# The first two modulation groups in quarters of their outputs, columns picked by four identity columns, first k-slice modulated on VectorE

## The reference, cut to what matters

```
mod = silu(c) @ w_mod + b_mod                # c for latent tokens, c_ctx for context tokens
shift1, scale1, gate1, shift2, scale2, gate2 = split(mod, 6)     # 1024 values each
h = layer_norm_plain(x) * (1 + scale1) + shift1
z = h @ w_in                                 # first 768 columns are q, k, v
```

## Time and profile before

| | |
|---|---|
| median of 3 runs | 936.22 us (934.71 to 936.78) |
| the profiled execution | 939.29 us, its span 937.5 us |
| TensorE busy | 869.9 us, 93% of the span |
| VectorE, ScalarE, GpSimd busy | 773.4, 581.3 and 158.5 us |
| mean granted TensorE clock | 0.967 |
| DMA | 272.78 MB, mean 291 GB/s |

### The profile page before, as it was taken

How to read it: one execution, slowest core, us unless ns; L and a number is a source line. 1 busy time by engine, 2 the same in 40 slices (tenths; PEclk the granted TensorE clock), 3 DMA queues, 4 the chain that set the end, 5 groups by cost and what they waited for, 6 DMA issues and landing times.

```text
span 937.5 us, 12308 instructions
## 1 busy us (share of the span) xinstructions
PE 869.9 (93%) x4962; PEld 613.7 (65%) x4962; DVE 773.4 (82%) x808; ACT 581.3 (62%) x596; POOL 158.5 (17%) x107
## 2 busy tenths in 40 slices
PE   3899999688899947999999999999999999999995
PEld 3789977456678834666666666666666666666663
DVE  5388545877879876898989989998998998998877
ACT  1455266746732344777777777777777777677753
POOL 1000300010011033003303303303302311320220
PEclk9899999799999966999999999999999999999998
DMA  9920540452059296999999999999999999999716
GB/s 338 361 110 8 201 181 1 180 105 78 2 204 357 93 400 247 373 419 392 418 392 393 410 392 390 402 398 388 390 402 385 378 415 381 374 414 386 268 15 201
DMA packets 59348, 272.78 MB, mean 291 GB/s; under 512 B 6728, under 2 KB 7036, under 8 KB 42908
## 3 DMA queue, kind: packets, MB, share of 16 engines
q1 hardware_dynamic: 50848, 245.33, 67.1%
q0 software_dynamic: 7536, 24.00, 9.0%
q10 hardware_dynamic: 908, 2.68, 0.8%
HBM read 257.99 MB, written 14.00 MB: 290 GB/s over the span
## 4 chain that ended last, share of the span: by engine, by line
PE 85%; DVE 6%; ACT 3%; DMA 3%; issue 1%; SPq 0%; another core or an unknown queue 0%; ACTq 0%; DVEq 0%
PE PS L935 24%; PE PS L937 24%; PE PS L936 24%; PE PS L1122 1%; PE PS L1076 1%; DMA ring<-in_w_mod 1%; PE PS L1106 1%; PE PS L1145 1%; PE PS L1262 1%; PE PS L1275 1%; DMA acc_scratch<-ysc,idx_u 1%; PE PS L1198 1%; DVE smin L1609 1%; PE PS L951 1%; PE PS L961 1%
## 5 line engine op out<-in xcount | busy, mean ns | idle before, releaser
L1788 DVE TENSOR_TENSOR Wl<-wr,Wh 128x2048 fp32r<-128x2048 f32 x190 | 432.7, 2290 | 51.6 <-ACT Wh L849 51.6
L849 ACT ACTIVATE Wh<-wr 128x2048 fp32r<-128x2048 f32 x192 | 367.5, 1915 | 68.9 <-PE PS L937 68.9
L935 PE MATMUL PS<-Wh,Xh 128*80 128x512 f32 x512 | 203.1, 397 | 1.3 <-ACT gate_act L871 0.8
L937 PE MATMUL PS<-Wl,Xh 128*80 128x512 f32 x512 | 201.7, 394 | 0.0
L936 PE MATMUL PS<-Wh,Xl 128*80 128x512 f32 x512 | 201.5, 394 | 0.0
L541 POOL DMA_INDIRECT acc_scratch<-ysc,idx_u x15 | 81.2, 5411 | 418.5 <-DVE ysc L1819 418.5
L937 PEld LDWEIGHTS PS<-Wl,Xh 128*80 128x80 f32 x512 | 76.0, 148 | 42.4 <-issue 0.5
L935 PEld LDWEIGHTS PS<-Wh,Xh 128*80 128x80 f32 x512 | 76.1, 149 | 41.9 <-issue 1.7
L936 PEld LDWEIGHTS PS<-Wh,Xl 128*80 128x80 f32 x512 | 76.1, 149 | 39.6 <-issue 0.5
L935 PE MATMUL PS<-Wh,HTh 128*80 128x512 f32 x256 | 101.6, 397 | 0.0
L936 PE MATMUL PS<-Wh,HTl 128*80 128x512 f32 x256 | 100.4, 392 | 0.0
(11 more groups left out here) (307 smaller groups left out, 1192.8 us busy)
## 6 DMA issues: line engine op xcount, KB each, us to landing
wr<-in_w_gate_up SPq DMA_DIRECT2D x128, 1024.0 KB, 10.5
wr<-in_w_down SPq DMA_DIRECT2D x64, 1024.0 KB, 9.7
ring<-in_w_mod SPq DMA_DIRECT2D x24, 1024.0 KB, 10.2
ring<-in_w_in SPq DMA_DIRECT2D x4, 1024.0 KB, 6.5
ring<-in_w_out SPq DMA_DIRECT2D x4, 1024.0 KB, 14.2
w_qkv<-in_w_in SPq DMA_DIRECT2D x4, 768.0 KB, 13.1
h_scratch<-h POOLq DMA_DIRECT2D x5, 512.0 KB, 5.8
acc_scratch<-xt POOLq DMA_DIRECT2D x5, 512.0 KB, 6.5
```

Source lines behind the costliest of these rows:

```text
L849: act.activation(Wh[n % NWH][:], wr[s][:], ACT.Copy).then_inc(W_hi, 1)
L935: pe.matmul(out, w[0], x[0], start=first, stop=False)
L937: return pe.matmul(out, w[0], x[1], start=False, stop=last)
L1788: dve.tensor_tensor(Wl[s][:], wr[s][:], Wh[n % NWH][:].bitcast(F32), ALU.subtract).then_inc(W_lo, 1)
```

## The change

- The 8 units are cut differently. Unit v now holds all 8 input slices for 256 of the outputs (a quarter), v even for shift1 and v odd for scale1. Quarter m = v // 2 gives the columns of k = 2m and 2m + 1. The size stays 1 MB; a row of the source is 1 KB where it was 2 KB. quarter_group does a unit in 32 instructions of 64 columns.
- The transfers are now ordered two units, one w_qkv, four times over.
- There are 8 row copies (128 by 64) instead of 4 (128 by 128), and 8 row transposes. A row transpose is now two small products of the copied row with four picked columns of the identity, so that the accumulator gets only the 4 columns that are used.
- Order: quarter 0 stands ahead of all x transposes, behind the small transpose of the parameter rows (which stood behind half_group(0)); quarter 1 behind chunk 1's; quarter 2 behind the last chunk. Quarters 3 to 7 stand in the loop's steps k = 0 to 4, between chunk 0 and chunk 1, and row transposes 3 to 6 at the ends of steps 0 to 3, 7 in step 4.
- On ScalarE the row copies 2 and 3 stand in step 0 and copies 4 to 7 at the ends of steps 1 to 4.
- Slice k = 0 is modulated by VectorE (two tensor_scalar), not by ScalarE. The rotary tables (16 small products, gtab) are made behind step k = 2 instead of ahead of the loop. Bias and modT are written two columns at a time.

The diff, cut to its core:

```diff
-        for hf in range(2):
-            for v in range(4 * hf, 4 * hf + 4):
-                g, _, ks, home = half_unit(v)
-                stream(v, home, w_mod_v[:, ks[0]:ks[0] + 4, g, H2 * hf:H2 * hf + H2])
-            for m in range(2 * hf, 2 * hf + 2):
-                sp.dma_start(w_qkv[:, 2 * m:2 * m + 2, 0:QKV], w_in_v[:, 2 * m:2 * m + 2, 0:QKV]).then_inc(w_qkv_in[m], 16)
+        for m in range(4):
+            for v in range(2 * m, 2 * m + 2):
+                stream(v, quarter_home(v), w_mod_v[:, :, v % 2, D4 * m:D4 * m + D4])
+            sp.dma_start(w_qkv[:, 2 * m:2 * m + 2, 0:QKV], w_in_v[:, 2 * m:2 * m + 2, 0:QKV]).then_inc(w_qkv_in[m], 16)
...
         mod_row_copy(0)
-        for c in range(CH):
+        xT_copy(0)
+        xT_copy(1)
+        mod_row_copy(1)
+        for c in range(2, CH):
             xT_copy(c)
-        mod_row_copy(1)
         for k in range(KC):
             act.wait_ge(w_qkv_in[k // 2], 16)
             split_w(k, w_qkv, QKV)
             if k == 0:
-                act.wait_ge(xT_ok, CH)
-            if k % 4 == 0:
-                act.wait_ge(modT_ok, 2 + k // 2)
-            act.activation(xnT[:, k, 0:N_S], xnT[:, k, 0:N_S], ACT.Identity,
-                           bias=modT[:, 0, 0, k:k + 1], scale=modT[:, 1, 0, k:k + 1])
...
-            if k == 3:
                 mod_row_copy(2)
                 mod_row_copy(3)
+            else:
+                if k % 2 == 0:
+                    act.wait_ge(modT_ok, k + 2)
+                act.activation(xnT[:, k, 0:N_S], xnT[:, k, 0:N_S], ACT.Identity,
+                               bias=modT[:, 0, 0, k:k + 1], scale=modT[:, 1, 0, k:k + 1])
...
+                if k <= 4:
+                    mod_row_copy(k + 3)
...
-        def half_group(v):
-            g, hf, ks, home = half_unit(v)
-            b = (2 * g, 4 + g)[hf]
+        def quarter_group(v):
+            out, home = quarter_banks(v)[0], quarter_home(v)
             landed_wait(pe, v)
-            for i, k in enumerate(ks):
+            if v in (2, 3):
+                pe.wait_ge(xT_ok, CH)
+            elif v >= 4:
+                pe.wait_ge(modT_ok, v - 1)
+            for k in range(KC):
                 for q in range(4):
-                    last = pe.matmul(PS[MG * q:MG * q + MG, 512 * b:512 * b + P], cT[:, k, :],
-                                     home[:, i, q * P:(q + 1) * P], start=(k == 0), stop=(k == KC - 1))
+                    last = pe.matmul(out[MG * q:MG * q + MG, :], cT[:, k, :], home[:, k, q * 64:(q + 1) * 64],
+                                     start=(k == 0), stop=(k == KC - 1))
             last.then_inc(mod_used, 2)
...
-        def row_transpose(n):
-            pe.wait_ge(mrow_ok, n + 1)
-            out = (bank(1, 0, P), bank(3, 0, P), bank(4, 256, 256 + P), bank(5, 256, 256 + P))[n]
-            pe.transpose(out, m_rowA[n][:], ident).then_inc(mrow_t, 1)
+        def row_transpose(v):
+
+            pe.wait_ge(mrow_ok, v + 1)
+            picks = ident.rearrange("p (a b m) -> p a b m", a=2, b=2)
+            for b in range(2):
+                last = pe.matmul(quarter_banks(v)[1][64 * b:64 * b + 64, :], m_rowA[v][:], picks[:, :, b, 0:2],
+                                 start=True, stop=True)
+            last.then_inc(mrow_t, 1)
...
-                if k == 3 and c == 0:
-                    row_transpose(3)
-            if k == 1:
-                half_group(4)
-                half_group(5)
-            if k == 2:
-                row_transpose(2)
-                half_group(6)
-                half_group(7)
+                if c == 0 and k == 0:
+                    row_transpose(2)
+                if c == 0 and k < 5:
+                    quarter_group(k + 3)
+                if c == 1 and k == 4:
+                    row_transpose(7)
+            if k < 4:
+                row_transpose(k + 3)
...
+            if k:
+                split_lo_w(k, w_qkv, QKV)
+                dve.wait_ge(hmod_ok, k)
+            else:
+                dve.wait_ge(modT_ok, 2)
+                dve.wait_ge(xT_ok, CH)
+                for s_, part_ in enumerate((slice(0, N_S), slice(N_S, NT))):
+                    last = dve.tensor_scalar(xnT[:, 0, part_], xnT[:, 0, part_], modT[:, 1, s_, 0:1], modT[:, 0, s_, 0:1],
+                                             ALU.mult, ALU.add)
+                link(last)
             link(dve.tensor_copy(Hh[:, k, :], xnT[:, k, :]))
             dve.tensor_tensor(Hl[:, k, :], xnT[:, k, :], Hh[:, k, :].bitcast(F32), ALU.subtract).then_inc(h_lo, 1)
+            if k == 0:
+                split_lo_w(k, w_qkv, QKV)
+            if k == 2:
+                rope_rows()
```

More of the change, by code:

```diff
@@ L225, in _build @@
     rows, grow, ones = at("rows", [P, P], Fz + 2048), at("grow", [1, P], Fz + 2560), at("ones", [1, P], Fz + 3072)
-    m_rowA = [at(f"m_rowA{n}", [P, P], Fz + 512 * n) for n in range(4)]
+    m_rowA = [at(f"m_rowA{n}", [P, 64], Fz + 256 * n) for n in range(8)]
     xnT = at("xnT", [P, KC, NT], Fz + 5120)
@@ L348, in _build, with quarter_home, quarter_banks @@
     U_R, U_MB, U_O, U_G = 8, 12, 24, 28
[L350 to L354, removed]
+    def quarter_home(v):
+        return ring[:, 2 * (v % 4):2 * (v % 4) + 2, :].rearrange("p a (b n) -> p (a b) n", b=4)
+    def quarter_banks(v):
+        b = (0, 2)[v] if v < 2 else 4 + v % 2
+        return bank(b, 0, 64), bank(b + 1, 0, 4) if v < 2 else bank(b, 256, 260)
     block = ctx.enter_context(nc.Block())
@@ L983, in _ @@
         pe.transpose(bank(3, P, P + R_END), rows[0:R_END, :], ident[0:R_END, 0:R_END]).then_inc(rows_t, 1)
-        half_group(1)
+        pe.wait_ge(ct_ok, 2)
+        quarter_group(0)
         row_transpose(0)
-        for c in range(3):
+        for c in range(2):
             x_transposes_of(c)
[L988 to L991, removed]
+        quarter_group(1)
         pe.wait_ge(cols_ok, 2)
         row_transpose(1)
+        for c in range(2, CH):
+            x_transposes_of(c)
+        quarter_group(2)
         def qk_transposes(c):
@@ L1392, in decay_rates, with mod_cols @@
             dve.tensor_scalar(nsp[:, 0, :], acc, -1.0, None, ALU.mult).then_inc(nsp_ok, 1)
-        def mod_cols(n, plus):
-            dve.wait_ge(mrow_t, n + 1)
-            w, hf = n % 2, n // 2
-            src = (bank(1, 0, P), bank(3, 0, P), bank(4, 256, 256 + P), bank(5, 256, 256 + P))[n].rearrange("p (q m) -> p q m", q=4)
-            lo = R_BM + 8 * w + 4 * hf
+        def mod_cols(v):
+            dve.wait_ge(mrow_t, v + 1)
+            w, k = v % 2, v - v % 2
+            src = quarter_banks(v)[1].rearrange("p (k m) -> p k m", k=2)
+            lo = R_BM + 8 * w + k
             for s_ in range(2):
-                last = dve.scalar_tensor_tensor(modT[:, w, s_, 4 * hf:4 * hf + 4], src[:, :, s_], plus, cols[:, lo:lo + 4],
+                last = dve.scalar_tensor_tensor(modT[:, w, s_, k:k + 2], src[:, :, s_], float(w), cols[:, lo:lo + 2],
                                                 ALU.add, ALU.add)
@@ L1408, in split_lo_w, with rope_rows @@
                               ALU.subtract).then_inc(split_lo, 1)
-        mod_cols(0, 0.0)
-        for g in range(2):
-            for w in range(2):
-                for c in range(PC):
-                    dve.tensor_tensor(gtab[:, g, w, c, :].rearrange("p (a b n) -> p a b n", a=2, b=2),
-                                      gqk[:, g, :].rearrange("p (a b n) -> p a b n", a=2, b=2),
-                                      rope[:, c, w, :].rearrange("p (a n) -> p a n", a=2).unsqueeze(2).broadcast_to([P, 2, 2, 16]),
-                                      ALU.mult)
-        mod_cols(1, 1.0)
-        for k in range(KC):
-            if k == 4:
-                mod_cols(2, 0.0)
-                mod_cols(3, 1.0)
-            split_lo_w(k, w_qkv, QKV)
-            dve.wait_ge(hmod_ok, k + 1)
+        def rope_rows():
+            for g in range(2):
+                for w in range(2):
+                    for c in range(PC):
+                        dve.tensor_tensor(gtab[:, g, w, c, :].rearrange("p (a b n) -> p a b n", a=2, b=2),
+                                          gqk[:, g, :].rearrange("p (a b n) -> p a b n", a=2, b=2),
+                                          rope[:, c, w, :].rearrange("p (a n) -> p a n", a=2).unsqueeze(2).broadcast_to([P, 2, 2, 16]),
+                                          ALU.mult)
+        mod_cols(0)
+        mod_cols(1)
+        for k in range(KC):
+            if k % 2 == 0 and k:
+                mod_cols(k)
+                mod_cols(k + 1)
+            if k:
[8 more added lines that the diff above has]
+                link(last)
             link(dve.tensor_copy(Hh[:, k, :], xnT[:, k, :]))
             dve.tensor_tensor(Hl[:, k, :], xnT[:, k, :], Hh[:, k, :].bitcast(F32), ALU.subtract).then_inc(h_lo, 1)
+            if k == 0:
+                split_lo_w(k, w_qkv, QKV)
+            if k == 2:
+                rope_rows()
         decay_rates()
```

12 lines of the change are left out of this document (5 added, 7 removed).

## The result

The changed kernel takes 943.85 us (median of 4 runs, 943.01 to 944.2), the kernel before 936.42 beside it. The ratio is 1.0082, with a 95% interval of 1.0068 to 1.0096: slower by 7.4 us. The profiled execution took 943.51 us, its span is 941.7.

What follows compares the result with a forecast made beforehand. TensorE, gapless from 60 us on, was taken as the bound, so the time follows when it finishes its k loop. -2.0 - 0.8 + 1.15 + 0.6 - 0.85 + 6.0 + 1.2 = +5.3 us on the 936.22 median gave 941.5, range 936.0 to 948.0.

Steps and rivals of the forecast that it cites:

- Part 4: Loop: row copies wait for the same step's quarter, so TensorE idles 1.5 us a step; +6.0 and +1.2 us.
- Part 1: Start: x transposes begin earlier, and TensorE starts k = 0 at 28.4 us; -2.0 us.
- Part 2: Clock around k = 0: the low spell comes again, with less of the work in it; -0.8 us.
- Part 3: TensorE's loop work: five quarters for four half groups +1.1 to 1.2, row transposes +0.6, old stall before k = 4 gone -0.85.
- The rival that it costs 1.9: Quarters: issue, not columns, sets their time, so each takes 1.9 us; +10.7 us, 947; chance 0.18.
- The rule of the Trainium skill: Quarters: matmuls never start closer than about 25 ns, so 64 records take 1.6 us and not 0.98.
- The rival "it gets faster": Loop: ScalarE's chain is covered and Parts 1 to 3 alone count; -1.9 us, 934.3; chance 0.10.
- The rival "the clock falls in the loop": Loop: TensorE's idle time brings low clock spells, one to two times; +2 to +4 us, 943.5 to 945.5; chance 0.15.
- The rival "both sizes fall small": Low spell before k = 0 goes entirely and stalls are 1.0 us a step; +0.9 us, 937; chance 0.12.
- What I called hidden: Loop: extra mod_cols pairs and rotary tables lie beside TensorE's work and cost nothing; up to 4 us if uncovered.

Runs made afterwards that it cites:

- experiment 1: The changed kernel with row copies 3 to 7 one step later on ScalarE and row transposes 3 to 6 one step later on TensorE: 937.67 us.
- experiment 2: The changed kernel with quarters 3 to 7 behind chunk 2 of their step, each followed by its row transpose: 962.22 us.
- experiment 3: The changed kernel with 34 added identity transposes on TensorE between 6 and 14.7 us, where it waits for its first weights: 940.95 us.
- experiment 4: The changed kernel with slice 0 modulated by ScalarE again and WAl of slice 0 ahead of Hh, as in the kernel before: 943.94 us.
- experiment 7: The changed kernel with row copies one step later, TensorE kept busy early by identity transposes, and slice 0's WAh ahead of row copy 1, WAl early: 937.12 us.
- experiment 9: The changed kernel with row copies one step later, TensorE kept busy early, slice 0's WAh behind row copy 1 and WAl behind quarter 1's columns: 936.45 us.
- experiment 10: The kernel of experiment 9 with 17 more identity transposes, 9 ahead of quarter 2 and 8 behind it: 937.09 us.
- experiment 12: The kernel before with 26 identity transposes ahead of half_group(0) and 24 ahead of the first product: 933.69 us.
- experiment 6: The changed kernel with row copies one step later and TensorE kept busy from 6 us on by identity transposes: 935.70 us.
- experiment 8: The kernel before with 34 identity transposes ahead of half_group(0): 934.83 us.
- experiment 11: The kernel before with 24 identity transposes between row transpose 1 and the first product: 933.95 us.

## Why the prediction was right

The sign, the mechanism of the loss and the range held: 941.5 forecast, 943.85 measured. Its four parts were less exact than their sum, and some of the agreement is luck, since errors of 2 to 3 us cancelled. By the steps of the text:

- **Part 4, the loop through ScalarE.** Shown. A step was to last 5.8 us and lasts 5.90; experiment 1 takes the loop apart and gives back 6.2 us, experiment 2 makes it longer and the step follows to 8.0. The chain was to be 3.6 us and is 3.55. What covers it was mis-sized: a step holds 4.87 us of work and not 4.3, so the idle time was 1.03 to 1.04 and not 1.5, and all waits of the loop were 5.0 us and not 7.2 (6.0 + 1.2). A chunk behind a wait or a quarter takes 1.15 to 1.26 us and not 1.05 (37.36 to 38.62 is one), and a row transpose takes 0.21.
- **Part 1, the start, -2.0.** In the profile of the changed kernel it was +0.8 (31.28 against 30.46). I had let only the first x chunk run at half rate. In this profile it was two, 3.68 us for 16 transposes, and quarter 1 as well, 1.94. The kernel before had worked on its first two half groups in that slow stretch, and the changed one has the x transposes there. But this start differs from one execution to the next: experiments 1 and 2 have the same lists ahead of the loop, and their first products come at 30.51 and 28.92 (0.05 and -1.5 against before), with 3.68 and 2.53 us for the same 16 transposes. So the 28.4 of the forecast is near the early ones, and the changed kernel's profile is a late one. That the slow stretch sets the start is shown by experiment 3: with the array busy from 6 us on the first product comes at 27.68.
- **Part 2, the clock, -0.8.** Before, 5.4 us of work lay in the low spell, 2.7 us lost; in the profile after there is no low spell in the loop, so the term was -2.7. Parts 1 and 2 are off by 2.8 and 1.9 in opposite directions, and they seem to be one thing: in experiments 1, 2 and 4, where the first product comes earlier, there is a low spell behind it. In experiment 4, whose loop is that of the changed kernel, the first product comes at 29.20 and chunk 0 is still reached at 68.47, next to the 68.62 of the changed kernel. What an earlier start gave, the clock took. Together the two parts were forecast at -2.8 and came to -1.9.
- **Part 3, the work.** A quarter takes 1.10 us at the full rate, with its drain; 1.08 was forecast. The rival that it costs 1.9 is refuted. It took 1.93 only in the slow stretch, as half group 0 had. The rule of the Trainium skill quoted in the prediction ("TensorE: Matmul & The Clock Gate", section "Wait — 56ns, not 53.3ns?") does not hold for this form in four column groups: 1.10 us for 64 records is 17 ns a record.
- **The rival "it gets faster"** would have had the chain covered. Experiment 1 covers it, and even then the kernel is at 1.0019. Its -1.9 rested on the -2.0 of Part 1.
- **The rival "the clock falls in the loop"** did not come in the profiled run, but experiment 2 shows it at gaps of 2.9 us.
- **The rival "both sizes fall small"** had both its conditions met in the profiled run: no low spell ahead of the loop, and stalls of 1.0 us a step. Its time of 937 did not come, because the start was 2.8 us later than in its sum and a step held some 0.5 us more work.
- **What I called hidden** was: in experiment 1 TensorE has no gap from 36 to 60 us, with the rotary tables, the waits for modT_ok and the later transfers all in place. The transfers cost what was estimated, 3.0 us a unit at 350 GB/s (3.1 forecast), and none of TensorE's waits within the loop is for one.

Of the 6.8 us at the mark, then: 0.8 start; waits for Hl, 5.0 against 0.85, +4.15; five quarters at 1.03 from start to start for two pairs of half groups at 1.88, +1.4; six row transposes of 0.21 for two, +0.8; -2.7 clock. That leaves some 2.3, which is the longer chunks, 10 or 11 of them at 0.1 to 0.2 more, some 1.7, and about 0.6 us that I cannot place. The other 0.6 between 6.8 and the median's 7.4 is within what the executions differ by, among other things in their clock.

What stays open: whether the stop within quarter 3 in experiments 7, 9 and 10 is a wait for instructions, and with it whether the quarters' layout, freed of its loop and of that stop, could beat the halves. In no run here does it.

## What to carry to other kernels

When a small item is moved into a loop of an engine that runs ahead, look at what it waits for. If that is produced in the same turn by the engine that is waiting for this one, the lead is gone, and each turn costs the whole chain; one turn later in the list costs nothing and gave back 6 us here. Read the idle time of the bound engine not only for its length but for what it does to the rate of the work behind it: filling 3 us of waiting with useless transposes gave the kernel before 2.2 us, and no form of the change that was tried beat the kernel before. It has to be measured each time: in experiment 10 such filling brought nothing, and in experiments 9 and 12 a filling at the start was followed by a low clock in the x transposes.

When one profile shows a start that is late or early by a us or two, look at other traces with the same lists ahead of that place before you give it a cause.

## What the runs showed of the hardware

- Where nothing fills the first waiting, the rows show a granted clock of 1.00 from 14 us on, but the work there ran at first at half the rate that it had later: 1.93 us for a group that takes 1.10. In the kernel before the last slow group ends at 18.87, in the changed one at 22.89, in experiment 2 at 16.32 with part of the x transposes behind it (2.53 us for 16 that take 1.97). With filling work ahead of it, the same group took 1.10 at once in experiments 3, 6, 7 and 9.
- The time of four matmuls in four column groups goes with their columns down to 64: 3.66 us for 64 records of 256 columns, 1.95 for 128, 1.10 for 64.
- A load of 1 KB rows moves 350 GB/s, of 2 KB rows 384, of 4 KB rows 409.
- Waiting of 1.9 to 3.0 us ahead of the loop was followed by a low clock in seven profiles (the kernel before, experiments 1, 2, 3, 4, 6 and 8), but not in that of the changed kernel (2.08 us). Filling it kept the clock at 1.00 in experiment 11.
- TensorE can stop inside a list of small matmuls with no wait in it, for 1.9 us, at a time when the transfers fill the queues (share 1.1). In a window of 5 us around that stop (experiment 7, 28 to 33 us) the profile lists one packet of the queue named instruction. The changed kernel has such a packet too and no stop; the timing told under experiments 7 and 9 is what speaks for a wait for instructions, and it was not tested.

```profile
q1 hardware_dynamic: 1576, 1.77, 108.3%
q8 instruction: 1, 0.02, 1.4%
```
